# A softmax stage in another order: scores behind the first head's turns, and a copy ahead of both shifts

## What is computed

```python
def block_attention(q, k, v):
    # q: (B, S, KV, G, Dk), k: (B, S, KV, Dk), v: (B, S, KV, Dv) -> (B, S, KV*G*Dv)
    ...
    def one(qblk):                      # 128 queries
        sc = jnp.einsum('bqkgc,bskc->bkgqs', qblk, k).astype(jnp.float32) * scale
        p = jax.nn.softmax(sc, axis=-1)
        return jnp.einsum('bkgqs,bskc->bqkgc', p.astype(v.dtype), v)
...
c_out = block_attention(q_c, k_c, v_c)              # "mla": keys of 64 + 32 (rope) numbers
d_out = block_attention(dq, dk, dv)                 # "gqa": keys of 64 numbers
return jnp.concatenate([c_out, d_out], axis=-1) @ w_out
```

## Time and profile before

| | us |
|---|---|
| three timed runs, median | 4221.75 |
| lowest and highest of them | 4216.45, 4222.77 |
| the profiled execution, own time | 4215.72 |
| its span, first to last instruction | 4214.0 |
| stage mla in it, first scores to last multiply | 3258.0 to 3477.9 |
| stage gqa in it, likewise | 3488.0 to 3678.1 |
| TensorE busy, of the span | 3713.1 (88%) |
| VectorE busy | 2456.5 (58%) |
| ScalarE busy | 1639.8 (39%) |

### The profile page before, as it was taken

The page is one execution under the profiler, slowest core; times in us unless marked ns, Lnnn a source line. Parts: engine busy times, 40 slices in busy tenths (PEclk is TensorE's granted clock), DMA queues, the critical chain, the costliest instruction groups (busy, mean ns, idle before and its releaser), DMA issues. The chain is left out here.

```text
span 4214.0 us, 58214 instructions
## 1 busy us (share of the span) xinstructions
PE 3713.1 (88%) x23176; PEld 3016.2 (72%) x23176; DVE 2456.5 (58%) x3914; ACT 1639.8 (39%) x2306; POOL 366.4 (9%) x233
## 2 busy tenths in 40 slices
PE   6988999978989999999798998599786998994996
PEld 3767777767777888887698776477685776773774
DVE  3366671568765555556332663777664666636785
ACT  5223432158320000003112763367434666623775
POOL 0011111000000000000000000144100000000442
PEclk9989999989999999999899999799898999996998
DMA  5011224530522111112223214499624103042997
GB/s 189 17 46 39 77 72 147 187 132 31 177 108 85 40 40 60 40 45 85 75 76 102 96 57 177 161 369 373 230 78 130 36 7 128 24 145 100 374 369 279
DMA packets 193583, 527.05 MB, mean 125 GB/s; under 512 B 27416, under 2 KB 126520, under 8 KB 174288
## 3 DMA queue, kind: packets, MB, share of 16 engines
q1 hardware_dynamic: 171424, 446.23, 29.3%
q0 software_dynamic: 18816, 75.62, 5.7%
q10 hardware_dynamic: 3120, 2.10, 0.2%
HBM read 432.52 MB, written 91.37 MB: 124 GB/s over the span
## 5 line engine op out<-in xcount | busy, mean ns | idle before, releaser
L2545 ACT ACTIVATE mlp_relu<-mlp_z 128x512 f32<-128x512 f32 x64 | 38.3, 599 | 633.5 <-PE mlp_z L157 633.5
L155 PE MATMUL scans_G<-ring_r 128*128 128x512 f32 x544 | 222.1, 408 | 32.3 <-ACT scans_stg L3092 18.3
L3667 DVE TENSOR_TENSOR ring_r<-ring,oN_r 128x4096 fp32r<-128x4096 f32 x48 | 212.4, 4425 | 63.6 <-ACT oN_r L3595 62.9
L3667 DVE TENSOR_TENSOR ring_r<-ring,hT_r 128x4096 fp32r<-128x4096 f32 x48 | 212.3, 4424 | 57.0 <-ACT hT_r L3595 57.0
L155 PE MATMUL mlp_z<-oN_r,mlp_w_high_r 128*128 128x512 f32 x512 | 203.0, 396 | 5.6 <-DVE ring_r L2586 5.6
L3595 ACT ACTIVATE oN_r<-ring 128x4096 fp32r<-128x4096 f32 x48 | 174.0, 3628 | 80.6 <-DMA ring<-in_w_all 68.7
L155 PE MATMUL mlp_y_ps<-mlp_w_high_r,ring_r 128*128 128x512 f32 x512 | 204.1, 399 | 0.0
L157 PE MATMUL mlp_z<-oN_r,ring_r 128*128 128x512 f32 x512 | 203.1, 397 | 0.0
L156 PE MATMUL mlp_z<-hT_r,mlp_w_high_r 128*128 128x512 f32 x512 | 202.3, 395 | 0.0
L157 PE MATMUL mlp_y_ps<-mlp_w_high_r,ring_r 128*128 128x512 f32 x512 | 201.8, 394 | 0.0
L156 PE MATMUL mlp_y_ps<-ring_r 128*128 128x512 f32 x512 | 201.4, 393 | 0.0
(11 more groups left out here) (683 smaller groups left out, 10165.8 us busy)
## 6 DMA issues: line engine op xcount, KB each, us to landing
ring<-in_w_all SPq DMA_DIRECT2D x110, 2048.0 KB, 10.7
ring<-in_w_mlp SPq DMA_DIRECT2D x16, 2048.0 KB, 8.4
ring<-in_w_all SPq DMA_DIRECT2D x12, 1024.0 KB, 6.2
branch_gates<-scans_stg SPq DMA_DIRECT2D x48, 256.0 KB, 2.0
merge_raw<-branch_gates SPq DMA_DIRECT2D x16, 768.0 KB, 5.1
diff_gemm_more<-in_w_all POOLq DMA_DIRECT2D x10, 1024.0 KB, 6.0
ring<-in_w_all POOLq DMA_DIRECT2D x6, 1024.0 KB, 6.1
ring<-in_w_even SPq DMA_DIRECT2D x4, 1536.0 KB, 6.6
```

The costliest lines, as they stand in the source:

```text
L155: pe.matmul(out, lh, rh, start=start, stop=False)
L2545: act.activation(r[:, n % 2, :], Z[:, n % 4, :], ACT.Relu).then_inc(z_free, 1)
L3667: dve.tensor_tensor(buf_r[:, b, :], buf[:, b, :], w_high[n % RING].bitcast(F32), ALU.subtract)\
```

## The change

In TensorE's loop body `turn` and the turn of head 0 of tile n move ahead of the scores of tile n + 1. In VectorE's the copy of head 0 of tile n moves ahead of the shift of head 0 of tile n + 1. ScalarE's and SyncE's code stays.

```diff
             for n in range(-1, N + 1):
+                def turn(hd):
+                    u = 2 * n + hd
+                    pe.wait_ge(exped, u + 1)
+                    for half in range(2):
+                        if u >= 1:
+                            pe.wait_ge((ev_act, ev_dve)[half], u)
+                        for k in range(4):
+                            kb = 4 * half + k
+                            ins = pe.transpose(TP[:, half, k, :], sc[:, u % 3, kb * P:(kb + 1) * P], m["ident"][:])
+                        ins.then_inc(t_done, 1)
+
+                if 0 <= n < N:
+                    turn(0)
                 if n + 1 < N:
                     p, qb = divmod(n + 1, NT)
...
-                def turn(hd):
...
-                if 0 <= n < N:
-                    turn(0)
                 if n >= 1:
                     w, g = n - 1, (n - 1) // 2
...
-                if n + 1 < N:
-                    shift(2 * n + 2)
                 if 0 <= n < N:
                     take(2 * n)
                 if n + 1 < N:
+                    shift(2 * n + 2)
                     shift(2 * n + 3)
```

## The result

The changed kernel takes 4256.19 us (median of 4 runs, 4251.6 to 4259.27), the kernel before 4221.18 on the same chip. The ratio is 1.0084, with a 95% interval of 1.0066 to 1.0101: 35.0 us slower, where 4250 and a range of 4242 to 4261 had been forecast. TensorE's new row costs what the forecast's main term said it would, and a little more.

A forecast was written before the change was run, and what follows sets the result against it. TensorE was taken to set the pace, as the sum of its start-to-start distances in each tile. The terms 29.0 - 1.5 + 2.8 gave +30.3 us, from which 4250 us was taken, range 4242 to 4261.

The forecast's parts named there:

- the forecast's main term: Both stages, every tile: second head's turns directly before the next tile's first-head turns cost 0.50 us more, +29.0 us.
- What bounds the stages: Middle of both stages: TensorE sets the pace; its four start-to-start distances sum to 6.54 us (mla), 5.63 (gqa) a tile.
- Part 1, the handover: Between consecutive tiles' turns sharing `TP`: turns wait for copies, 1.43 us start to start; 0.50 a tile, +29.0 us.
- Rival (c): Gap behind each tile's scores is a wait for ScalarE's exponential and goes: 0.16 us a tile, 4231 us; 4%.
- Part 2, nothing later than the handover: Each tile's chain of scores, shift, exponential, turn stays in time: cost 0, margin 0.27 us.
- Rival (b): ScalarE's copy of the second head's turns is late in each tile: 13 us more, 4263 us; 9%.
- Part 3, the pair changes: Three times a stage, where VectorE splits the next pair's operands, the delay shrinks: together -1.5 us.
- Part 4, the start: Start of each stage, TensorE at half clock in mla: +1.3 us mla, +1.5 gqa, +2.8 together, bounds +0.6 and +4.6.
- The sum: Whole kernel: 29.0 - 1.5 + 2.8 = +30.3 us, bounds +28.1 and +32.1; 4250 us taken.
- Rival (a): TensorE's clock falls around the adjoining turns and wait in each tile: 87 us if every tile, 4337 us; 3%.
- (d): Faster: gap behind scores goes and the wait between adjoining turns hides under start-up, down to 4202 us; 2%.
- (e): TensorE's row: the build puts the pieces as before, nothing moves, 4221 us; 1%.

The follow-up runs named there:

- The row T0, S, T1, V with four pieces: Kernel before with TensorE's order first head's turns, next scores, second head's turns, values; rounding and split in four pieces: 4225.3 us, ratio 1.0012.

## Why the prediction was right, step by step

- **What bounds the stages** held: TensorE's distances added up to the tile before and after, and most of what the tile gained (0.50 of 0.58) is the one distance that changed.
- **Part 1, the handover**, was read off the end of the mla stage at 1.43 us, and is 1.43 in the middle of mla and 1.44 in gqa, with 31 waits in each stage, nearly all of 0.34 us. The term, 0.50 a tile and 29.0 us, was too small by 0.08: 0.58 and 0.57 were measured, 16.7 + 16.5 = 33.2 us. The missing piece is R: the forecast let V behind the scores take the 2.10 us that it takes behind a turn. A lone turn between scores and values takes 0.26 to the next start for 0.20, and T0 to S and S to V came out 0.01 longer each. With R moved behind T0 the tile was 0.16 shorter.
- **Rival (c)**, that the gap behind the scores was a wait for the exponential and would go, did not come true: S to R is 2.50 and 1.59 with the same 0.36 ahead of the weights and "issue" as its releaser. The 33 times that the profile named ScalarE in gqa were no wait for it.
- **Part 2, nothing later than the handover**, held in the change: ScalarE idle for 0.24 where 0.27 was laid out. Rival (b) did not come. The row T0, S, T1, V with four pieces shows such a wait in gqa, where the shift comes 0.8 us late: T0 waits 0.32 for an exponential.
- **Part 3, the pair changes**: 7.27 for 7.12 in mla (0.15, forecast 0.35), none in gqa (forecast 0.15). Before they had cost 1.7 and 1.2 us in all, so -2.5 us instead of -1.5: the term was too small by 1.0, the other way from the rest.
- **Part 4, the start**: forecast +1.3 and +1.5, measured +4.3 and +1.4 in this profile. (For mla the forecast's own working gives +1.1; the +1.3 that it takes is the middle of its bounds.) The step that failed is the bound for mla, 2.3. It had the scores of tile 1 at 1.2 GHz at worst, but not that the clock would fall again in the idle time behind T1(0), which that same paragraph had laid out (T0(1) to R(0) 4.92 us for 3.53), nor that the first scores of all would end at 1.2 GHz as well (their second part 1.65 us for 1.05). With TensorE's part alone the same start came out at +1.7, inside the bound, so how far off this term was is in part chance. That gqa's +1.5 was hit is one profile too; its other one says +1.9.
- **The sum**: 33.2 - 2.5 + 5.7 + 0.1 (ends) = 36.5 in the profile, 30.3 forecast; on the medians 35.0. The tile (+4.2) and the start (+2.9) were too small and the pair changes (-1.0) took a part of that back. The forecast of 4250 was 6 us low.
- **Rival (a)** did not come in mid-stage; **(d)** needed the gap to go, and it didn't; **(e)**, that nothing moves, is out with 31 waits a stage.

## What to carry to other kernels

Two pieces of work of one engine that fill the same PSUM banks want another piece between them that lasts as long as the others take to empty the banks; here 0.69 + 0.74 us from start to start, read off the one place in the old trace where they already stood together. When a row of a saturated engine is rewritten, add up its distances start to start for each pair of neighbours that is new, small ones too: here the turn of the reciprocals cost 0.20 us behind other turns and 0.26 behind scores, and that made up most of what the forecast of the tile missed. And whatever stands ahead of the copy that empties a bank (a rounding once a pair) becomes part of the handover: here it was 1.6 us, three times a stage.

## What the runs showed of the hardware

- At mla's start the clock fell in a pause of 2.15 us, just after it had come up: 1.00 at 3274 to 3276, 0.50 at 3277. In the kernel before it fell at the end of one of 2.47 us. A pause of 2.14 us at gqa's start, also just after the clock had come up, left it at 1.00 (T0 1.07 us). In mid-stage, waits of 0.34 us in each tile, with two groups of turns next to each other, left it at 1.00.
- TensorE's row here has small fixed distances: 0.36 us ahead of the weights behind the scores' shapes, 0.17 behind the turns' and the values', with no one waited for. They stay when the row is rewritten.
- VectorE's and TensorE's parts of one change cost 11.6 and 34.7 us alone and 35.0 together: here what a move cost depended on the other engine's row.
- In the profile's page for a tile, a releaser by name can stand for a gap that has nothing to do with it: "ACT gqa_sc, 11.3, 33 times" was the same 0.36 us that stands behind the scores in mla and in the changed kernel, where "issue" is named.
